# Block 1's gates as x (1 + tanh(x / 2)), multiplied from the bank, with their gating and transposes in a step queue of their own

## The reference: what is computed

```python
h = jnp.einsum('bsd,de->bse', x, w_in)
(dq, dk, dv, sq, sk, sv, iq, ik, iw, fq, fk, fv, ff, gate) = split_columns(h)
...
a = a * lax.rsqrt(jnp.mean(a * a, axis=-1, keepdims=True) + SUBLN_EPS) * g_subln.astype(jnp.float32) * (1.0 - lambda_init)
...
mixed = jnp.concatenate([a, bo, co], axis=-1) * jax.nn.silu(gate.astype(jnp.float32))
out = jnp.einsum('bse,ed->bsd', mixed.astype(x.dtype), w_out)
return layer_norm(DEEPNORM_ALPHA * x + out, ln_g, ln_b)
```

## Time and profile before

| | us |
|---|---|
| median of 3 runs | 1402.99 |
| range of the runs | 1400.14 to 1403.83 |
| the profiled execution | 1403.85 |
| its span, first to last instruction | 1402.5 |
| TensorE busy (94% of the span) | 1318.3 |
| VectorE busy | 865.4 |
| ScalarE busy | 594.3 |
| GpSimd busy | 278.2 |
| mean granted clock of TensorE | 0.964 |

### The profile page before, as it was taken

One profiled execution on the slowest core, in us unless ns is written; L12 is line 12 of the kernel. 1 busy time (PEld: TensorE's weight loads), 2 busy tenths in 40 slices (PEclk: granted clock), 3 DMA queues, 4 the chain that ended last, 5 costly groups with the idle time before them and its releaser, 6 DMA issues.

```text
span 1402.5 us, 18894 instructions
## 1 busy us (share of the span) xinstructions
PE 1318.3 (94%) x7490; PEld 1041.7 (74%) x7490; DVE 865.4 (62%) x1484; ACT 594.3 (42%) x983; POOL 278.2 (20%) x217
## 2 busy tenths in 40 slices
PE   7999887989979899997999999999999998799998
PEld 5777776867767777775777877777888876578876
DVE  4694646784578643488997532324586678845553
ACT  3444442444474455222434532223463563346442
POOL 0200102210022322237100011311252142201112
PEclk9999988999989999998999999999999998989998
DMA  7571566275253411111111122222553333123451
GB/s 250 213 256 57 181 224 210 91 254 182 91 181 111 158 61 52 55 61 61 62 59 45 61 90 90 91 90 90 156 175 95 106 106 93 57 77 121 147 177 66
DMA packets 49192, 168.46 MB, mean 120 GB/s; under 512 B 5862, under 2 KB 7078, under 8 KB 48848
## 3 DMA queue, kind: packets, MB, share of 16 engines
q1 hardware_dynamic: 49104, 167.26, 35.9%
HBM read 166.19 MB, written 1.05 MB: 119 GB/s over the span
## 4 chain that ended last, share of the span: by engine, by line
PE 72%; DVE 11%; issue 11%; POOL 4%; ACT 1%; DMA 1%; SPq 0%; POOLq 0%; DVEq 0%; ACTq 0%
PE bank L1467 15%; PE bank L1468 15%; PE bank L1469 15%; PE bank L1386 4%; PE bank L1780 3%; PE bank L1485 3%; DVE conv_val L2523 3%; DVE w_lo L2210 2%; PE bank L1486 2%; PE bank L1487 2%; PE bank L1755 1%; PE bank L1547 1%; PE bank L1510 1%; PE bank L1716 1%; PE bank L1463 1%
## 5 line engine op out<-in xcount | busy, mean ns | idle before, releaser
L1467 PE MATMUL bank<-w_hi,x_hi 128*128 128x512 f32 (+4 forms) x1120 | 466.0, 416 | 13.2 <-DVE w_lo L2210 8.0
L2210 DVE TENSOR_TENSOR w_lo<-w_raw,w_hi 128x1024 fp32r<-128x1024 f32 (+3 forms) x264 | 320.6, 1218 | 252.1 <-ACT w_hi L1817 251.8
L1817 ACT ACTIVATE w_hi<-w_raw 128x1024 fp32r<-128x1024 f32 (+3 forms) x264 | 270.1, 1027 | 439.3 <-PE bank L1469 263.4
L1468 PE MATMUL bank<-w_lo,x_hi 128*128 128x512 f32 (+4 forms) x1120 | 437.7, 391 | 0.0
L1469 PE MATMUL bank<-w_hi,x_lo 128*128 128x512 f32 (+4 forms) x1120 | 437.3, 390 | 0.0
L1467 PEld LDWEIGHTS bank<-w_hi,x_hi 128*128 128x128 f32 x1120 | 216.4, 193 | 65.0 <-DVE w_lo L2210 11.4
L1469 PEld LDWEIGHTS bank<-w_hi,x_lo 128*128 128x128 f32 x1120 | 214.6, 192 | 46.9
L1468 PEld LDWEIGHTS bank<-w_lo,x_hi 128*128 128x128 f32 x1120 | 215.7, 193 | 39.4
L2523 DVE SCALAR_TENSOR_TENSOR conv_val<-conv_u,par,conv_val 128x512 f32<-128x512 f32 (+1 forms) x240 | 150.3, 675 | 0.0
L2843 POOL TENSOR_TENSOR merged<-merged,sigma 128x512 f32<-128x512 f32 x24 | 37.4, 1586 | 178.9 <-DVE sigma L2565 178.9
L1485 PE MATMUL bank<-x_hi,w_hi 128*128 128x512 f32 (+1 forms) x192 | 68.0, 354 | 0.5 <-ACT conv_val L2020 0.5
(11 more groups left out here) (331 smaller groups left out, 1759.0 us busy)
## 6 DMA issues: line engine op xcount, KB each, us to landing
w_raw<-in_w SPq DMA_DIRECT2D x172, 512.0 KB, 3.5
w_raw<-in_wm SPq DMA_DIRECT2D x48, 512.0 KB, 5.0
w_raw<-in_wo SPq DMA_DIRECT2D x40, 512.0 KB, 3.5
w_raw<-in_wy_gla SPq DMA_DIRECT2D x8, 512.0 KB, 3.5
w_raw<-in_wy_conv SPq DMA_DIRECT2D x8, 512.0 KB, 3.5
...
```

Source lines behind the costliest of these rows:

```text
L1467: mm(out, xh[:, q, col], hi[:, kk, 0:w], start=q == 0 and not with_bias, stop=False)
L1468: mm(out, xh[:, q, col], lo[:, kk, 0:w], start=False, stop=False)
L1817: do(hi, raw, ACT.Copy).then_inc(sem["cut_hi"], 1)
L2210: v.tensor_tensor(lo, raw, hi.bitcast(F32), ALU.subtract).then_inc(sem["cut_lo"], 1)
```

## The change

There are three parts.

1. `ev1` of a gate chunk takes Tanh(x / 2) where it copied. Behind it `gate_silu`, now on VectorE, computes (tanh + 1) times the bank's x, and it is this step that gives the bank free. `gate_mul` takes a factor of 0.5 with it (silu(x) = 0.5 x (1 + tanh(x / 2))). ACT's six silus of a layer and their table load are gone; `table_of` tells the planner that a gate's `ev1` wants the tanh table, which is at hand in the set that the exponentials use.
2. Gating and transposes leave `first_main` for a queue `mixed(l)`: for g = 0, 1, 2 and each tile `gate_mul`, then `flip mix`. The planner may place them anywhere that their own conditions allow.
3. In block 2's layer 0 the branches are merged in the order 1, 2, 0 where it was 1, 0, 2, with the waits that follow from it.

```diff
-BRANCHES = [(1, 0, 2), (1, 0, 2)]
+BRANCHES = [(1, 2, 0), (1, 0, 2)]
...
-    gates = [("gate_silu", l, g, each) for g in range(3) for each in range(NT)] if (c, t) == (GB, NT - 1) else []
+    gates = [("gate_silu", l, MIX_CHUNK.index(c), t)] if c in MIX_CHUNK else []
...
-    for g in (0, 1):
-        for t in range(NT):
-            yield [("gate_mul", l, g, t)]
-        for t in range(NT):
-            yield flip("mix", l, t, g)
     yield from project("out1", l, 0, range(NT), residual, range(NP - 1))
-    for t in range(NT):
-        yield [("gate_mul", l, 2, t)]
-    for t in range(NT):
-        yield flip("mix", l, t, 2)
     yield from project("out1", l, 0, range(NT), residual, range(NP - 1, NP))
     yield from project_by_tile("out1", l, 1, range(NT), residual)
     yield from layer_norm(l)
+
+
+def mixed(l):
+
+    for g in range(3):
+        for t in range(NT):
+            yield [("gate_mul", l, g, t)] + flip("mix", l, t, g)
...
-        for side in (sparse, fox_gates, diff, fox):
+        for side in (mixed, sparse, fox_gates, diff, fox):
...
-            do(m.gate[:, t, 0:512], ps[:, :], ACT.Copy).then_inc(sem["ev1"], 1)
+            do(m.gate[:, t, 0:512], ps[:, :], ACT.Tanh, scale=0.5).then_inc(sem["ev1"], 1)
...
-    def gate_silu(l, g, t):
-        part = m.gate[:, t, MIX_COLS[g]]
-        act.wait_ge("ev1", l, MIX_CHUNK[g], t)
-        do(part, part, ACT.Silu).then_inc(sem["gate_silu"], 1)
...
+    def gate_silu(l, g, t):
+        part = m.gate[:, t, MIX_COLS[g]]
+        ps = k.bank[slot("proj", "in1", l, MIX_CHUNK[g], t)[0]]
+        dve.wait_ge("ev1", l, MIX_CHUNK[g], t)
+        v.scalar_tensor_tensor(part, part, 1.0, ps[:, (0, 0, 256)[g]:(512, 256, 512)[g]], ALU.add, ALU.mult).then_inc(sem["gate_silu"], 1)
...
-        v.tensor_tensor(part, part, m.gate[:, t, MIX_COLS[g]], ALU.mult).then_inc(sem["gate_mul"], 1)
+        v.scalar_tensor_tensor(part, part, 0.5, m.gate[:, t, MIX_COLS[g]], ALU.mult, ALU.mult).then_inc(sem["gate_mul"], 1)
```

50 lines of the change are left out of this document (30 added, 20 removed).

## The result

| | before | the change |
|---|---|---|
| median of 12 runs each, us | 1401.59 | 1404.22 |
| range of the runs | 1397.38 to 1403.83 | 1401.14 to 1407.45 |
| ratio, with its 95% interval | | 1.0023 [1.0013, 1.0033] |
| span of the profiled execution | 1402.5 | 1404.2 |

The change makes the kernel about 3.2 us slower (0.0023 x 1401.6; the medians are 2.6 apart). The forecast was +6.4 us on the profiled execution: the sign is right, the size is twice too large, and 1409 lies outside the change's own runs.

What follows compares the result with a forecast made beforehand. Time falls only where TensorE waits (84.2 us) or its clock is down. Layer 0 -7.0, layer 1 +13.9, branches and tables 0, less half a microsecond for early GLA steps: +6.4, so 1409 us, range 1397 to 1417.

Steps and rivals of the forecast that it cites:

- Layer 0: End of `in1`: waits fall from 5.77 to 2 us (3.8), clock 2.5, wait before GA's kp 2 0.7; sum -7.0.
- The clock term: Layer 0, first twelve matmuls of `out1`: half clock after the waits costs 2.9 us, of which 2.5 would go.
- The length from `ev1` to kp 3: Layer 1, GB's last `ev1` to tile 1's kp 3 of `out1`: 12.9 us longer, kp 3 at 436.2 instead of 423.3.
- 8.5 for the landing: Layer 1: late `sub_sum` delays `sub_end`, so SP loads context later and the bias table lands 8.5 us later, at 414.2.
- 4.4 for the stream: Layer 1: VectorE's stream from the table's landing to tile 1's kp 3 grows from 17.6 to 22.0 us.
- a side remark: Layer 1, ScalarE: `bias_sel` holds `flip_hi` of g = 1 and `out1`'s cut until the table lands; some 5 us idle.
- Part 3, 0: Block 2's layer 0: TensorE has no idle time, so the new branch order gains 0, bounds -1 and +1.
- VectorE's added work: Twelve multiplications from the bank, 6.1 us over two layers, count only where VectorE itself is last, in layer 1.
- The table load: ScalarE: each load priced at the row's 1.28 us, without the skill's drain, which would give layer 0 1.4 more.
- The strict order of a queue: ScalarE, VectorE and GpSimd queues are strictly first in, first out, which speaks against the change in layer 1.
- C: Rival, near no change: landing 8.5 late, but the 4.4 us longer VectorE stream vanishes into waits; 1405.5, chance 0.17.
- B: Rival, faster: GB's `ev1` some 6 us earlier against the attentions, so the context load isn't late; 1399, chance 0.18.

Runs made afterwards that it cites:

- e11: The change's gates in both layers, with gating and transposes back in the layer's own queue instead of `mixed`; 0.9955 of the kernel before.
- e8: The kernel before with the new queue `mixed` alone, its copies and ScalarE silus kept, branches as before; 1.0097 of the kernel before.
- e4: The change with one planner condition added: weight cut 129 on VectorE stands behind `sub_sum` of layer 1's tile 1; 1.0044 of the kernel before.
- e7: The change with the old queue in layer 1 only, new gates in both layers; 0.9970 of the kernel before.
- e5: The kernel before with one more SP wait, so context and bias table load only after layer 1's `gate_mul` (g = 1, tile 1); 1.0065, 1408.22 us.
- e15: The change with layer 1's context transposes and `bias0` behind the mix's last flips, and the planner's context load time 8.0, not 4.0; 0.9968 of before.
- e12: The kernel before with only the new branch order 1, 2, 0 in block 2's layer 0; 0.9998 of the kernel before.
- e6: The change with weight cut 129 behind `sub_sum` of tile 1 and layer 1's mix transposes behind `fox`'s last `att_v`; 1.0070 of the kernel before.
- e9: The change with weight cuts 129 to 131 behind the load's conditions and layer 1's mix transposes behind `fox`'s last `att_v`; 1.0020 of the kernel before.
- e1: The kernel before with the new gates and queue in layer 0 only, old branch order; 0.9965 of the kernel before, 1394.84 us.
- e10: e9's planner conditions put on e7, so the old queue in layer 1; 0.9953 of the kernel before.
- e16: e11 with the planner's estimate of the context load at 8.0 us where it was 4.0; 0.9973 of the kernel before.

## Why the prediction was off, and where it was right

The chain of the profiled pair, stretch by stretch in time, against the forecast:

| stretch | forecast | measured |
|---|---|---|
| ahead of GA's kp 2 | -0.7 | -0.3 |
| layer 0, T0 | -6.3 | -7.6 |
| layer 1, up to GB's last `ev1` | none | -3.2 |
| from there to kp 3 of tile 1 | +12.9 | +12.7 |
| from there to T1's end | +1 | +1.5 |
| the rest | -0.5 | -1.4 |
| sum | +6.4 | +1.7 |

- **Layer 0: right in size and in its main cause, with one term wrong.** Waits of 2 us were forecast to stay and 1.8 did, so they fell by 4.0 where 3.8 was forecast. This gain is the silus' going, as the root on ScalarE had said, and not the new queue: e11 has it without the queue, e8 has the queue and loses 2.8 in T0. The clock term was mis-sized. It put 2.5 us on the first twelve matmuls of `out1`. From the first to the thirteenth it was 199.13 - 193.89 = 5.2 us, and is 190.26 - 185.81 = 4.5: 0.8 less. (The 2.9 it started from is too high as well: 0.63 and 0.39 are durations of matmuls that overlap, and they start 0.43 and 0.23 apart, which makes 2.4 for twelve.) What made up for it is the 3.8 us of busy time ahead of `out1`, the clock there and the attention steps that moved out, and that this came to nearly the same sum is luck.
- **The forecast's missing term** is the third line of the table, and it is the step that failed: the sum followed the loss at layer 1's end, started it at GB's last `ev1` as if that stood where it did, and put the stretch ahead of it at nothing without a reason. Attention steps of `fox`, tile 1, moved from ahead of GB's last projections to behind them, into waits that were there anyway, and some idle time ahead went too. The windows from layer 1's start to the end of the last `ev1`, before and after, columns as above, show it:

```profile
234.16:397.53 163.37, 158.85 (x1030) 125.72 (x1030) 107.19 (x239) 71.64 (x154) 22.81 (x15) 0.96 0.45 156
```

```profile
226.30:386.43 160.13, 156.57 (x1021) 124.08 (x1022) 105.04 (x236) 69.86 (x153) 19.31 (x13) 0.96 0.47 163
```

  TensorE has 158.85 - 156.57 = 2.3 us less work there and 4.5 - 3.6 = 1.0 less idle time (4.52 and 3.56), at the same clock, so the last `ev1` comes 3.2 us earlier. The other runs repeat it, and show that it is the gates' doing and not the queue's: this stretch is 162.4 to 163.5 us in the five kernels with layer 1's silus kept (e8, with the queue, 162.4) and 159.1 to 161.0 in all others (e11, without it, 159.1). Against the +3.2 of twelve runs this term alone is the size of the miss; the rest of the table's difference, 1.5 us, is within what two profiled executions differ by.
- **The length from `ev1` to kp 3: right to 0.3 us, in part by luck.** 38.7 was forecast (16.7 to the landing, 22.0 behind it), 38.4 measured (17.4 and 21.0). But the forecast had all of the 12.9 as idle time of TensorE, from 8.8 to 21.7. It idles 16.6: 4.8 of the growth is busy time, in part the attention steps that came from ahead of the `ev1`. Counted from the start of layer 1, the table lands 6.0 us later than before, where the forecast took 8.5.
- **Its cause: half wrong.** The forecast split it into 8.5 for the landing and 4.4 for the stream, and said that the landing hangs on `sub_end`. In the trace `sub_end` did come 8.8 us later against the last `ev1` than before (8.95 and 0.12 behind it). But `att_out` of `fox` is the last condition in the kernel before (over at 397.98, `sub_end` at 397.65) and holds the load nearly as long in the change, as e4 shows. And e7 and e11 show a landing as late as the change's with T1 only 1.8 to 2.4 us above that of before: 7.3 of the 12.7 us go with the queue. Adding a delay to a length holds where the path runs through it, as e5 shows for the kernel before; in the change's order the path runs through the order of the streams, of which e15 gives back 7.0 us. What the forecast had as a side remark, that `bias_sel` stands ahead of `flip_hi` of g = 1 though nothing of theirs depends on it, is one of the two pieces of order that e15 mends.
- **Part 3, 0: right** (e12, 0.9998).
- **VectorE's added work: right that it has no price of its own.** e11 has all of it and gains 6.3 us. Its busy time grew by 4.4, where 6.1 of multiplications were counted.
- **The table load.** The forecast went by the row's 1.28 us and not by a drain of 1380 ns on top, which the Trainium skill, "ScalarE: Activation LUTs", section "What ACT_TABLE_LOAD costs", counts. With the drain layer 0 would have gained 1.4 more than 7.0, an estimate by that page. The trace of before shows no time for it: the `ev1` ahead is over at 183.76, the load begins at 183.78, and the first silu at 185.08. The waits fell by 4.0 where the row's price gave 3.8. T0 fell by 7.6, which by itself would not exclude 1.4 more, since two profiled executions differ by more.
- **The strict order of a queue** was the right place to look. The Trainium skill, "PSUM — Partial Sum Buffer", section "Engine vs sequencer instructions", states it for ScalarE, VectorE and GpSimd. The trace agrees: `flip_hi` of g = 1 begins at 408.21 in the change, behind `bias_sel` and its wait. e15 adds the price, 0.55% for the two blocked places together.

Among the rivals, C's time (1405.5) is nearest to the result and its mechanism isn't what happened: b did grow, by 3.5. B's was that the last `ev1` comes early against the attentions; it did come 3.2 us early, but the landing came late all the same, since `sub_sum` and `att_v` moved with it.

What stays open: what the landing as early as before would be worth in the new queue, and how much of the +12.7 is the late landing where the two pieces of order aren't mended (e4, e6 and e9 moved other steps along with it). e15 still holds 3.9 us in T1 against before, which no run took apart.

Six kernels (e1, e7, e10, e11, e15, e16) are faster than both the one before and the change, by intervals that end below 0.9985. The simplest is e11, the gates alone, 0.9955 [0.9937, 0.9972], 1395.38 us.
